# A state-space stage on one core: gate tiles moved between the kernel products and ahead of the states

## The reference

```python
def hybrid_layer(x, w_in, ...):
    proj = jnp.einsum('bsd,de->bse', x, w_in)
    q, c_kv, q_idx, k_idx, w_idx, gate_a, u, gate_s = jnp.split(proj, _split_points(), axis=-1)
    att = dsa_attention(q, c_kv, q_idx, k_idx, w_idx, kv_g, w_uk, w_uv)
    ssm = s5_branch(u, log_dt, a_re, a_im, b_re, b_im, c_re, c_im, d_skip, w_glu, b_glu)
    mixed = jnp.concatenate([att * jax.nn.silu(gate_a), ssm * jax.nn.silu(gate_s)], axis=-1)
    y = jnp.einsum('bse,ed->bsd', mixed, w_out)
    return layer_norm(DEEPNORM_ALPHA * x + y, ln_g, ln_b)

def s5_branch(u, ...):       # 32 groups of 16 channels, each with 64 complex states
    ...
    _, states = lax.associative_scan(_ssm_combine, (a_seq, bu), axis=1)
    y = jnp.einsum('bsgp,gcp->bsgc', states, c_mat).real + d_skip * u32
    y = jax.nn.gelu(...)     # then a GLU
```

## Time and profile before

| what | value |
|---|---|
| time, median of 3 runs (lowest, highest) | 2488.62 us (2487.3, 2489.1) |
| time of the profiled execution | 2487.84 us |
| its span, first to last instruction | 2486.0 us |
| PE busy | 2385.3 us, 96% of the span |
| DVE busy | 1448.4 us, 58% |
| ACT busy | 837.4 us, 34% |
| POOL busy | 405.4 us, 16% |
| mean granted TensorE clock | 0.987 of full speed |

### The profile page before, as it was taken

The page is one execution under the profiler, slowest core; times in us unless marked ns, Lnnn a source line. Parts: engine busy times, 40 slices in busy tenths (PEclk is TensorE's granted clock), DMA queues, the critical chain, the costliest instruction groups (busy, mean ns, idle before and its releaser), DMA issues.

```text
span 2486.0 us, 31700 instructions
## 1 busy us (share of the span) xinstructions
PE 2385.3 (96%) x12809; PEld 1789.7 (72%) x12809; DVE 1448.4 (58%) x2275; ACT 837.4 (34%) x1470; POOL 405.4 (16%) x631
## 2 busy tenths in 40 slices
PE   6999999999999999999999999999899999999997
PEld 6887888888777798788888887785556554745553
DVE  5567876332233466577834222325689999777762
ACT  5345555131113244455633111321441113422331
POOL 0034320000000001433000000000533952401011
PEclk9999999999999999999999999999999999999998
DMA  6010002122212310100031222214001011200000
GB/s 212 30 52 1 1 1 61 36 52 51 51 60 102 119 50 18 35 2 1 2 94 26 51 51 51 83 53 145 35 10 35 1 44 44 101 17 35 18 34 17
DMA packets 106385, 116.88 MB, mean 47 GB/s; under 512 B 20704, under 2 KB 78784, under 8 KB 106240
## 3 DMA queue, kind: packets, MB, share of 16 engines
q1 hardware_dynamic: 105088, 110.66, 14.4%
q10 hardware_dynamic: 1152, 4.19, 0.4%
HBM read 96.82 MB, written 16.84 MB: 46 GB/s over the span
## 4 chain that ended last, share of the span: by engine, by line
PE 83%; DVE 12%; ACT 2%; issue 1%; DMA 1%; POOL 0%; SPq 0%; DVEq 0%; POOLq 0%; ACTq 0%
PE PS L658 7%; PE PS L718 7%; PE PS L724 7%; PE PS L721 7%; PE PS L509 6%; PE PS L682 5%; PE PS L1105 5%; DVE R2a L2274 3%; DVE ssc L2273 3%; PE PS L771 2%; PE PS L1074 2%; PE PS L861 2%; PE PS L787 2%; PE PS L790 2%; PE PS L784 2%; PE PS L1052 2%
## 5 line engine op out<-in xcount | busy, mean ns | idle before, releaser
L721 PE MATMUL PS<-hLo,R2bR 128*128 128x512 f32 x768 | 298.8, 389 | 0.0
L718 PE MATMUL PS<-hHi,R2bR 128*128 128x512 f32 x752 | 293.1, 390 | 0.0
L724 PE MATMUL PS<-hHi,R2bR 128*128 128x512 f32 x752 | 292.6, 389 | 0.0
L1962 DVE TENSOR_TENSOR R2bR<-W,R2bR 128x1024 fp32r<-128x1024 f32 x48 | 57.5, 1221 | 267.3 <-ACT R2bR L1453 267.3
L1520 ACT ACTIVATE R3a<-PS,pT 128x512 f32<-128x512 f32 x64 | 42.3, 687 | 403.6 <-PE PS L724 403.6
L861 PE MATMUL PS<-hT,W 128*128 128x512 f32 x384 | 166.0, 593 | 0.8 <-ACT R L1601 0.8
L721 PEld LDWEIGHTS PS<-hLo,R2bR 128*128 128x128 f32 x768 | 144.3, 188 | 29.8
L1941 DVE TENSOR_REDUCE negm<-PS 128x1 f32<-128x1024 f32 x128 | 156.3, 1221 | 16.2 <-PE PS L658 15.5
L1469 ACT ACTIVATE R2b<-PS,negm 128x1024 f32<-128x1024 f32 x128 | 142.5, 1113 | 61.3 <-DVE negm L1941 61.2
L718 PEld LDWEIGHTS PS<-hHi,R2bR 128*128 128x128 f32 x752 | 141.3, 188 | 29.7 <-issue 0.5
L724 PEld LDWEIGHTS PS<-hHi,R2bR 128*128 128x128 f32 x752 | 141.2, 188 | 29.4
(11 more groups left out here) (405 smaller groups left out, 5207.5 us busy)
## 6 DMA issues: line engine op xcount, KB each, us to landing
W<-in_w_in SPq DMA_DIRECT2D x10, 2048.0 KB, 8.3
W<-in_w_in SPq DMA_DIRECT2D x33, 512.0 KB, 4.7
xres<-R SPq DMA_DIRECT2D x3, 4096.0 KB, 19.0
W<-in_w_out SPq DMA_DIRECT2D x6, 2048.0 KB, 8.6
R<-xres SPq DMA_DIRECT2D x2, 4096.0 KB, 18.4
R<-in_x ACTq DMA_DIRECT2D x8, 512.0 KB, 7.1
W<-in_w_in SPq DMA_DIRECT2D x4, 1024.0 KB, 9.6
R3a<-rsums SPq DMA_DIRECT2D x16, 256.0 KB, 5.2
```

Of the source, the lines that this page charges most:

```text
L718: mm = pe.matmul(o, wHi[c % 2][:, k, :], hi, start=(k == 0), stop=False)
L721: mm = pe.matmul(o, wHi[c % 2][:, k, :], hLo[:, k, ns], start=False, stop=False)
L724: mm = pe.matmul(o, wLo[c % 2][:, k, :], hi, start=False, stop=(k == 7))
```

## The change

It moves gate tiles in TensorE's list and, to match, their silu and one wait in ScalarE's list. No instruction is added or removed. Tile 1 of `gates(3)` goes from behind both kernel products to between them; tile 2 goes from between the states and the outputs to ahead of the states; tile 3 alone is left between states and outputs. The wait for the Toeplitz transfers moves with tile 2 (banks 4 and 5).

```diff
@@ TensorE
             gates(3, 0, (0,))
             s5_kernel(2)
+            gates(3, None, (1,))
             s5_kernel(3)
-            gates(3, None, (1,))
+            gates(3, None, (2,))
             s5_states(2)
             s5_states(3)
-            gates(3, None, (2, 3))
+            gates(3, None, (3,))
             s5_outputs(2)
             s5_outputs(3)
@@ ScalarE
             silu_gates(4, range(0, 2))
             s5_kernel(2)
+            silu_gates(4, range(2, 4))
             s5_kernel(3)
-            silu_gates(4, range(2, 4))
+            for p in range(2):
+                act.wait_ge(s2_TT[p], 16 * CL * 2)
+            silu_gates(4, range(4, 6))
             s5_states(2)
             s5_states(3)
-            for p in range(2):
-                act.wait_ge(s2_TT[p], 16 * CL * 2)
-            silu_gates(4, range(4, 8))
+            silu_gates(4, range(6, 8))
             s5_outputs(2)
             s5_outputs(3)
```

## The result

The changed kernel takes 2496.28 us (median of 6 runs, 2494.07 to 2503.5) against 2488.53 us before (6 runs, 2486.78 to 2489.1). The ratio is 1.004 with a 95% interval of 1.0029 to 1.0052: slower by 7.7 us, as forecast in sign; 2499.0 was the forecast, 2495.3 to 2503.5 the range.

A forecast was written before the change was run, and what follows sets the result against it. TensorE was taken as the bound, busy 2385.3 of 2486.0 us, waiting at the second pair's outputs. Profiled 2487.84 + 9.3 shift + 1.7 clock = 2498.8, stated as 2499.0; range 2495.3 to 2503.5.

The forecast's parts named there:

- The idle time between the kernel products: TensorE between kernels 2 and 3: 2.73 us idle and 1.2 us slow clock go, at most 3.9 us gained.
- The tile ahead of the states as the cost: TensorE before the states: one tile more, 13.91 us, less 3.9 saved, so the states start 10.0 us later.
- The chain: States through rotate, scan and rotate_back on GpSimd and VectorE to outputs(3): outputs(3) come 9.3 us later.
- ScalarE's moved wait: ScalarE's wait for Toeplitz transfers ahead of the states: costs nothing, 4 us of cover; 4 in 100 that it bites, 2500 to 2502.
- rival 1: GpSimd loses turns to six scans beside rotate(3), which takes 2.0 us more: 2501 us; 6 in 100.
- rival 2: VectorE's scans run freely, rotate_back(2) 0.9 us earlier, shift 7 to 8.4 us: 2497 us; 5 in 100.
- The clock term: Slow TensorE clock at outputs(3) after the new waits: 1.7 us taken, bounds 0 to 4.6.
- the lower bound: TensorE at outputs(3): no clock loss, if the clock has recovered during outputs(2) and holds.
- the forecast as costed: Whole kernel by the costed steps, clock term between 0 and 4.6: 2497.1 to 2502.5 us, 82 in 100.
- VectorE's lateness: VectorE's select resumes about 9.3 us later; costs nothing unless it exceeds TensorE's lateness by 7.4 us.
- The Trainium skill's rule: VectorE and GpSimd instructions on SBUF exclude each other for a whole instruction; taken both ways, 2501 us, not 2498.8.

The follow-up runs named there:

- experiment 1: Kernel before with only tile 1 moved between the kernel products, nothing ahead of the states, tiles 2 and 3 behind them; 2486.02 us against 2486.65.
- experiment 2: Kernel before with tiles 1 and 2 ahead of the states, none between the kernel products, tile 3 behind the states; 2501.93 us against 2486.65.
- experiment 3: Changed kernel with only half of tile 2 (bank 4, eight matmuls) ahead of the states, the other half behind; 2494.24 us, ratio 1.0031 to before.
- experiment 4: Changed kernel in which scan(2) on VectorE also waits for rotate(3) to end; 2497.15 us, ratio 1.0044 to before.
- experiment 5: Kernel before with tile 1 between the kernel products, none ahead of the states, and scan(2), scan(3) three select(5) steps earlier; 2480.94 us against 2487.01.

## Why the prediction was right, point by point

- **The idle time between the kernel products.** Predicted: 2.73 us and 1.2 us of slow clock gone, 0.76 us moved ahead of the tile. Measured: the gap of 0.76 us where predicted, and from the start of tile 1 to that of tile 2 2005.12 − 1988.33 = 16.79 us, 16.75 predicted. The states start 10.05 us later, 10.0 predicted, and 3.87 us earlier in experiment 1, where the extra tile is missing.
- **The tile ahead of the states as the cost.** Shown by experiments 1 and 2: the two halves of the change have opposite signs, −3.07 and +13.07 us, and their sum, 10.0, is near the 9.41 of both together. The difference of 0.6 us arises in front of the scans (0.8, less 0.2 at the states). Where the states are late, 0.63 and 0.64 us of it are absorbed there (13.70 against 13.07, 10.05 against 9.41; 0.7 predicted). Where they are early, VectorE's list keeps 0.80 us back (3.87 against 3.07).
- **The chain.** Predicted shift of outputs(3) +9.3 us, measured +9.41; VectorE's wait 6.8 us, measured 6.91; GpSimd's wait ahead of rotate_back(2) 1.0 us, measured 1.11; TensorE's wait ahead of outputs(2) 9.8 us, measured 9.75.
- **ScalarE's moved wait** costs nothing in the changed kernel and 2.2 us as soon as half the cover is gone (experiment 3). The transfers land 7.5 us behind the K16 copies; I had reckoned with up to 8.8.
- **The other rivals.** GpSimd did not lose turns: rotate(3) took 7.97 us with six scans beside it, where rival 1 had 2.0 us more. The scans did not run freely either: rotate_back(2) starts 1.11 us behind rotate(3), where rival 2 had it 0.9 us earlier than costed.
- **The clock term** was the one that was mis-sized: 1.7 us predicted, 0 in the profiled execution. Windows of TensorE over outputs(2) and outputs(3) after:

```profile
2046.60:2050.30 3.70, 3.67 (x16) 3.49 (x16) 3.56 (x8) 0.00 (x0) 2.89 (x5) 0.50 0.00 0
...
2055.20:2060.00 4.80, 4.01 (x48) 3.72 (x48) 4.63 (x8) 0.71 (x2) 0.00 (x0) 1.00 0.01 3
```

  outputs(2) take the slow clock (0.50), inside their own wait, and it costs nothing there. Because they take it they last 5.9 us instead of 3.95, the second wait is 2.75 us instead of some 4.7, and outputs(3) run at 1.00. It was the lower bound that I had named, "if the clock has recovered during outputs(2) and holds". I went by the row of the same stage instead, in which 2.73 us of idle time had brought the clock down. Experiment 3, with 4.62 us, paid 1.6. So a low clock at outputs(3) was possible, and the length of the wait may have decided it, but no run shows the rule: 2.53 to 2.75 us behind slow outputs(2) kept the full clock in three kernels, 2.73 us between the kernel products did not.
- **What lies outside the stage.** Without the clock term my sum is 2497.1; the profiled execution took 2495.01. The difference lies ahead of the stage, which begins at 1985.46 instead of 1987.78, 2.3 us earlier. Windows of before, then of after, at the start of the second block, where the two kernels are the same:

```profile
1700.00:1720.00 20.00, 17.77 (x58) 9.79 (x59) 14.04 (x59) 2.40 (x4) 0.00 (x0) 0.74 1.06 292
```

```profile
1700.00:1720.00 20.00, 17.11 (x64) 9.76 (x65) 12.62 (x51) 2.39 (x4) 0.00 (x0) 0.91 1.05 286
```

  A mean clock of 0.91 against 0.74 let TensorE do 64 matmuls instead of 58 in 20 us. The other traces agree: in the four with a clock of 0.80 to 0.91 in this stretch the stage starts at 1985.1 to 1985.9, in the four with 0.67 to 0.74 at 1987.6 to 1988.5. The kernels do not differ there, so this is not the change's doing.
- **The number was partly luck.** I forecast +10.4 us (2499.0 against 2488.62) and the medians moved by 7.7. The band that I gave the forecast as costed began at 2497.1, without the 0.78 us that its upper end contains; with them it would begin at 2497.9. The median, 2496.28, lies below both, in the part of the range that I had added for rival 2, which did not happen. The six executions spread over 9.4 us, so their median places the forecast only roughly, and against the 16 later runs of before the change costs 9.6 us. What bears the prediction out is the positions in the trace, not the number.
- **VectorE's lateness** cost nothing: its idle time in front of the first attention step is 7.41 us after and 7.42 before.

  Its row after:

```profile
2173.49 0.29 DVE L2381 CUSTOM_DVE_ANT_0 R3b<-PS,R2a 128x128 f32<-128x128 f32 x1 [7.41 <-PE PS L1053]
```

- **The Trainium skill's rule** on the pair of SBUF ports (SBUF — State Buffer, "Who interferes with whom"), whichever issues first blocks the other, is borne out on VectorE's side (a scan takes 1.42 us beside a GpSimd operation, 0.39 alone) and hardly on GpSimd's: 0.04 us for a scan in experiment 4.

## What to carry to other kernels

Work that can stand anywhere (a filler, here a gate tile) has a different price on either side of a long chain through other engines. In front of the chain's first step it delays everything that the chain feeds. Behind that step it runs while the chain runs and costs nothing. Moved from behind to ahead, a tile cost nearly its whole length once: 13.07 us for 13.7 in experiment 2. The idle time that it leaves behind is where the loss shows, not a second loss. So before filling a gap, ask on which side of the chain the filler stood: the tile for the 2.7 us gap stood ahead of the states already and could be had for nothing (experiments 1 and 5). Where a chain crosses an engine whose list is written by hand, that list has to move with it, or part of the gain stops at its next fixed place: 0.80 us here (experiment 1).

## What the runs showed that I had not expected

The granted clock makes a few microseconds of difference between executions of kernels that are the same in that place. In the stretch from 1700 to 1720 us the mean clock was 0.74 in one execution and 0.91 in another, and the stage behind it began 2.3 us earlier. From gates(4) to the end, 433.10 us in one execution stood against 429.85 in another with the same instructions and a higher clock (experiment 1 and before). A gain of 3 us in the stage, seen to the hundredth in the trace, did not show in a median of eleven runs; it shows again when executions with the same mean clock are compared. Why the clock differs from one execution to the next stays open. An idle time of 2.5 to 2.75 us ahead of outputs(3) was followed by the full clock in three kernels (the changed one, experiments 2 and 4), whereas the same length between the kernel products was followed by 0.50; 4.62 us (experiment 3) was followed by the low clock.
